# A two-layer diffusion step on one core: norms multiplied in by a diagonal matrix, one modulation unit moved between two layers, ring slots taken in the order in which they come free

## The chip, the cores and the metric

The kernel runs on one core of a Trainium2 chip. The metric is the device time of one execution in microseconds. Three executions of the kernel before took 1282.77, 1283.19 and 1284.61 us, median 1283.19 us. All data is fp32.

## The reference, cut to what matters

Two groups of 128 tokens (a prompt, t = 0, and a sample, t = 1) of width 1024 pass two layers. Each layer has an attention sub-layer and a mixture of 16 experts. Each sub-layer begins with an RMS norm whose result is shifted and scaled by values from a "modulation" product, and ends with a gated residual:

```
m   = silu(cond) @ w_mod[l] + b_mod[l]           # 6 x 1024: shift, scale, gate, twice
h   = x * rsqrt(mean(x*x) + eps) * g * (1 + scale) + shift
x   = x + gate * sublayer(h)                     # attention + projections, then top-2 of 16 experts
```

Weights are read once from HBM, 488 MB in all, most of it the experts' `w_gate`, `w_up` and `w_down`.

## The kernel before, in words

**Weights.** All weights go through a ring of six SBUF slots of 2 MB (`ring`, `SLOTS`). The dense units of a layer are listed by `dense_units(l)`: "mod" units (a quarter of the rows of `w_mod` for one group of 2048 columns), "in" units (512 columns of the input projection) and "out" units (512 columns of the output projection). SyncE issues their loads in that list's order (`load(g)`, L464 for a mod unit, L466 for the others). Unit g takes the slot of unit g - 6 and waits until TensorE has read that one (`read_at(g - SLOTS)`). The experts' units then take the same slots in turn: `load_first` (waits for the last six dense units), `load_early`, and the loops `load_in_turn`. Their DMAs are all issued at L475. The unit that TensorE has read is told by the semaphores `mod_used`, `filled` and `moe_used`.

**Order of the work.** TensorE works through one fixed order of jobs. In the dense part it is written out by hand in `FILL[l]`: at points called "head", "keys", "scores", and for each of the eight turns j of the attention before (`(j,)`) and after (`j`) its product with the values. Each turn is transposed probabilities (L699), scores of a later turn (L812), values (L849, L855 or L863). The items are ("in", u, t) = `project` (L752), ("wo", u, t) = `out_project` (L770), ("mod", l, group, k) = `mod` (L721, accumulated over k = 0..3 in one bank), ("hT", kind, t) = `norm`, ("rt", t) = `logits` (L875). Ahead of "head" the order is in the code: `project(l, 0, 1)`, `norm(l, 0, 0)`, then `project` of u = 1, 2, 3.

**A norm.** There are eight: (l, kind, t), kind 0 ahead of the attention and kind 1 ahead of the experts. ScalarE squares x and sums it (L1137 for 1024 columns at once; for (l, 1, 0) in two halves at L1133). VectorE asks for mean + eps (L1355, or L1386 and L1388 with halves). GpSimd raises it to the power -1/2 (L618). VectorE multiplies all of x by that number into scratch (`normed_rows`, L1395). TensorE transposes the scratch, eight 128x128 blocks into two PSUM banks (`norm`, which calls `transposes`, L699). ScalarE scales and shifts the first bank into `hT` (`modulate`, L1144) and VectorE the second (L1402). Only then can the product that reads `hT` start.

**Experts.** Eight pairs of experts per layer: `gather` (L932), `product` (L971), `scatter` (L941). The last pair is unrolled, with `last_product` and `last_scatter` (L1014). After it VectorE adds the four quarters (t, u) in `add_last`: a product with the gate (L1711, which counts `y_added`) and the sum into x (L1713, which counts `x_ready`).

**Between the layers.** VectorE runs `add_last` for (t = 1, u = 0), (1, 1), (0, 0), then asks for the norm of t = 1, then `add_last` of (0, 1), then `normed_rows(1, 0, 1)`, and the same for t = 0. ScalarE squares t = 1, then t = 0, and only then modulates t = 1. TensorE runs `mod(1, 1, 0)`, waits for `y_added` of all four quarters, and runs `norm(1, 0, 1)` and `project(1, 0, 1)`.

Of the kernel before, what the change touches and what calls it, by code (L numbers as in the profile page):

```python
# [12 lines left out]
D = 1024  # L13
# [89 lines left out]
def turn(l, j):  # L103
# [5 lines left out]
    0: {"head": [("in", 4, 1), ("in", 0, 0), ("in", 1, 0)],  # L109
# [13 lines left out]
    1: {"head": [("in", 4, 1), ("in", 5, 1)],  # L123
# [4 lines left out]
        2: [("mod", 1, 1, 1)],  # L128
        3: [("mod", 1, 1, 2), ("mod", 1, 1, 3)],
# [26 lines left out]
def dense_units(l):  # L156
# [4 lines left out]
    return shifts[0:1] + inputs + shifts[1:4] + scales[0:2] + out + scales[2:4]  # L161
# [14 lines left out]
def psum_jobs():  # L176

    names = [("vecT",), ("bT",)]
    for l in range(LAYERS):
# [7 lines left out]
        add( ("in", 0, 1), ("hT", 0, 0), ("in", 1, 1), ("in", 2, 1), ("in", 3, 1))  # L187
# [28 lines left out]
def build(nc, a):  # L216
    ctx = ExitStack()
    with ctx:
# [29 lines left out]
        ss = sb("ss", [P, 4])  # L248
# [111 lines left out]

        powers = {}
# [24 lines left out]
        N0 = len(dense_units(0))  # L386
        unit_no = {u: i for i, u in enumerate(units)}

        def dense_slot(g):

            return (g if g < N0 else g - OUTSIDE) % SLOTS

        MOE_AT = [N0 % SLOTS, dense_slot(len(units))]
# [23 lines left out]
        def read_at(g):  # L417

            if units[g][0] == "mod":
                l, group, k = units[g][1:]  # L420
                return mod_used, 12 * l + 4 * group + k + 1
            kind, l, u = units[g]
            return filled, fill({"in": ("qkv", l, u, 0), "out": ("wo", l, u, 0)}[kind])
# [34 lines left out]
        def _(sp):  # L458
# [9 lines left out]
            def experts(l):  # L468
# [8 lines left out]
                def load_in_turn(k, at, wait):  # L477
                    slot = (MOE_AT[l] - OUTSIDE + k) % SLOTS
# [4 lines left out]
                def load_early(n, k):  # L483
                    o = ring_turn(n, k)
                    slot = (MOE_AT[l] + o) % SLOTS
# [9 lines left out]
                def last_units(n):  # L495
# [4 lines left out]
                    for half in range(2):  # L500
                        for e in range(2):
                            k = MOE_UNITS - 2 + e
                            slot = (MOE_AT[l] - OUTSIDE + k) % SLOTS
# [88 lines left out]
            for g in range(N0, len(units)):  # L592
# [3 lines left out]
                else:  # L596
                    sp.wait_ge(*read_at(g - SLOTS))
# [80 lines left out]
        def _(pe):  # L678
# [241 lines left out]
            def experts(l):  # L920
# [23 lines left out]
                def product(n, k, banks, lhs, ready, half_done=None):  # L944
# [5 lines left out]
                    slots = [0, 0] if kept else [(MOE_AT[l] + turn_of + e) % SLOTS for e in range(2)]  # L950
# [883 lines left out]
```

## Time and profile before

| | |
|---|---|
| median of three executions | 1283.19 us |
| the profiled execution | 1283.81 us |
| its span | 1282.0 us |
| TensorE busy (PE) | 1183.7 us, 92% |
| VectorE, ScalarE, GpSimd busy | 279.4, 188.4, 49.4 us |
| bytes moved | 491.62 MB, mean 383 GB/s |
| matmuls of the experts' products (L971) | 638.6 us busy |

The span runs from the first to the last instruction; the execution's own time is 1.81 us longer. In 1 of the page (busy time by engine) PE is busy nearly all the time. In 2 of the page (40 slices) the DMA engines move about 427 GB/s in most slices, and far less in slices 2 and 3 and 21 to 24, the dense parts of the two layers.

### The profile page before, as it was taken

Reading aid. Unit: us, or ns where it says so; the run is one execution under the profiler, and the core shown is the slowest. Engines: PE = TensorE matmul, PEld = TensorE weight load, DVE = VectorE, ACT = ScalarE, POOL = GpSimd, SP = SyncE. Lnnn points to the kernel's source line nnn. Section 1 sums busy time; section 2 is a strip of 40 time slices with the busy share of each in tenths; the row PEclk is TensorE's granted clock in tenths of the full one; section 3 lists DMA queues with packets and bytes.
Section 4 is the critical chain, followed back from the end, with each engine's and each line's share of the span. In section 5 each row is a group of like instructions: output and inputs, shape, how many; then the busy total and the mean of one; then the engine's idle time right before and its main releaser. Section 6 shows DMA issues by size and latency. Waiting matters only on the chain.

```text
span 1282.0 us, 13868 instructions
## 1 busy us (share of the span) xinstructions
PE 1183.7 (92%) x5519; PEld 517.6 (40%) x5519; DVE 279.4 (22%) x672; ACT 188.4 (15%) x437; POOL 49.4 (4%) x57
## 2 busy tenths in 40 slices
PE   4999989999889898989899999999998899889898
PEld 2545454343333334333344554743433334343333
DVE  1156441201021010101413433412020110101013
ACT  1234221000000100000121342210000001000010
POOL 0502000000000000000011100000000000000000
PEclk9999999999999999999989999899999999999999
DMA  9959999999999999999991579889999999999995
GB/s 376 333 201 386 423 408 424 429 392 427 430 428 427 430 427 430 428 427 429 408 330 57 207 279 415 324 353 424 374 429 427 429 427 429 429 427 430 427 428 230
DMA packets 57647, 491.62 MB, mean 383 GB/s; under 512 B 5090, under 2 KB 6258, under 8 KB 26884
## 3 DMA queue, kind: packets, MB, share of 16 engines
q1 hardware_dynamic: 55408, 485.92, 91.4%
q0 software_dynamic: 2016, 4.94, 1.3%
q8 instruction: 29, 0.48, 0.1%
q10 hardware_dynamic: 180, 0.17, 0.0%
q14 instruction: 14, 0.11, 0.0%
HBM read 488.26 MB, written 2.75 MB: 383 GB/s over the span
## 4 chain that ended last, share of the span: by engine, by line
PE 72%; DMA 18%; issue 5%; DVE 2%; ACT 1%; SPq 1%; POOL 1%; DVEq 0%; ACTq 0%; POOLq 0%
PE bank L971 42%; DMA ring<-in_w_gate 11%; PE bank L752 11%; DMA ring<-in_w_up 5%; PE bank L770 3%; PE bank L941 3%; PE bank L932 3%; DMA ring<-in_w_in_ab 2%; PE bank L721 2%; PE bank L699 2%; PE bank L992 1%; PE bank L1021 1%; PE bank L812 1%; PE bank L1005 1%; PE bank L875 1%
## 5 line engine op out<-in xcount | busy, mean ns | idle before, releaser
L971 PE MATMUL bank<-ring,hT 128*64 128x512 f32 x2816 | 638.6, 608 | 63.7 <-issue 30.0
L971 PEld LDWEIGHTS bank<-ring,hT 128*64 128x64 f32 x2816 | 213.3, 140 | 464.5 <-issue 462.7
L752 PE MATMUL bank<-ring,hT 128*128 128x512 f32 (+1 forms) x352 | 149.5, 583 | 4.7 <-DMA ring<-in_w_in_ab 2.4
L752 PEld LDWEIGHTS bank<-ring,hT 128*128 128x128 f32 x352 | 67.1, 193 | 80.0 <-issue 76.6
L1694 DVE TENSOR_TENSOR work<-work,bank 128x512 f32<-128x512 f32 x56 | 38.5, 687 | 193.6 <-PE bank L941 193.4
L1687 DVE TENSOR_TENSOR work<-work,bank 128x512 f32<-128x512 f32 x32 | 22.0, 687 | 236.5 <-PE bank L971 236.5
L1728 DVE COPY work<-bank 128x512 f32<-128x512 f32 x16 | 11.1, 692 | 225.6 <-PE bank L971 209.3
L932 PE MATMUL bank<-work 128*128 128x128 f32 x512 | 59.8, 275 | 0.0
L932 PEld LDWEIGHTS bank<-work 128*128 128x128 f32 x512 | 58.6, 192 | 0.0
L770 PE MATMUL bank<-ring,work 128*128 128x512 f32 x128 | 56.3, 594 | 0.0
L1274 ACT ACTIVATE hT<-bank 128x512 f32<-128x512 f32 x32 | 19.0, 595 | 248.3 <-PE bank L1021 248.3
L941 PE MATMUL bank<-work 128*128 128x512 f32 x112 | 51.8, 605 | 0.0
L721 PE MATMUL bank<-ring,cond 128*32 128x512 f32 x384 | 47.0, 623 | 1.6 <-DMA ring<-in_w_mod 1.2
L1300 ACT ACTIVATE work<-bank 128x512 f32<-128x512 f32 x16 | 9.6, 597 | 220.3 <-PE bank L971 193.0
L1675 DVE TENSOR_TENSOR work<-work,bank 128x512 f32<-128x512 f32 x32 | 22.0, 688 | 83.4 <-ACT work L1283 83.4
L971 PE MATMUL bank<-work,hT 128*64 128x512 f32 x152 | 39.2, 593 | 0.0
L770 PEld LDWEIGHTS bank<-ring,work 128*128 128x128 f32 x128 | 23.8, 190 | 28.7 <-issue 28.6
L1287 ACT ACTIVATE work<-bank 128x256 f32<-128x256 f32 x16 | 6.2, 385 | 196.4 <-PE bank L1040 196.4
L1283 ACT ACTIVATE work<-bank 128x512 f32<-128x512 f32 x32 | 19.1, 597 | 94.5 <-PE bank L971 94.5
L941 PEld LDWEIGHTS bank<-work 128*128 128x128 f32 x112 | 20.1, 189 | 31.5 <-issue 31.5
L1211 ACT ACTIVATE work<-bank,nm 128x256 f32<-128x256 f32 (+1 forms) x64 | 26.1, 421 | 29.9 <-DVE nm L1486 29.9
L1420 DVE TENSOR_REDUCE hss<-bank 128x8 f32<-128x512 f32 (+1 forms) x16 | 10.5, 657 | 88.8 <-ACT bank L1170 88.8
(195 smaller groups left out, 688.5 us busy)
## 6 DMA issues: line engine op xcount, KB each, us to landing
ring<-in_w_gate SPq DMA_DIRECT2D x64, 2048.0 KB, 17.0
ring<-in_w_up SPq DMA_DIRECT2D x56, 2048.0 KB, 17.2
ring<-in_w_down SPq DMA_DIRECT2D x56, 2048.0 KB, 16.9
ring<-in_w_mod SPq DMA_DIRECT2D x23, 2048.0 KB, 11.9
work<-in_w_up SPq DMA_DIRECT2D x8, 2048.0 KB, 17.8
ring<-in_w_in_c SPq DMA_DIRECT2D x6, 2048.0 KB, 20.2
ring<-in_w_in_ab SPq DMA_DIRECT2D x4, 2048.0 KB, 21.5
ring<-in_w_down SPq DMA_DIRECT2D x8, 1024.0 KB, 16.3
```

What stands on the lines that cost most here:

```text
L699: ins = pe.transpose(b[:, i * P:(i + 1) * P], src, K("ident"))
L721: ins = pe.matmul(out, cond[:, 2 * k + r, :], cols, start=(k, r) == (0, 0), stop=(k, r) == (3, 1), tile_position=(0, 32 * j))
L752: ins = pe.matmul(b[:, 0:n], hT[:, c, t * P:(t + 1) * P], w[:, c, 0:n], start=c == 0, stop=c == DC - 1)
L770: ins = pe.matmul(b[:, :], oT(l, t, c), w[:, c, :], start=c == 0, stop=c == DC - 1)
L932: ins = pe.matmul(bank[h][:, c * P:(c + 1) * P], htok(t)[:, at:at + P], pick[:, t, :], start=t == 0, stop=t == 1)
L941: pe.matmul(bank[4 + 2 * t + h][:, :], GT[:, t, :], yd[:, h * UC:(h + 1) * UC], start=True, stop=True).then_inc(m["scattered"], 1)
L971: ins = pe.matmul(bank[banks[j]][64 * e:64 * e + 64, :], lhs[:, 4 * h + c, 64 * e:64 * e + 64], weights(e, c, j), start=(h, c) == (0, 0), ...
L1211: ins = act.activation(PR[:, j % 2, h, 0:nk], bank_of(("S", l, t, b, e))[:, i * nk:(i + 1) * nk], ACT.Exp, bias=nm[:, j % 2, h:h + 1], sca ...
L1283: act.activation(sg[:, h * UC:(h + 1) * UC], bank[h][:, :], ACT.Sigmoid).then_inc(m["sig_done"], 1)
L1675: dve.tensor_tensor(hid[:, half], sg[:, half], bank[h][:, :], ALU.mult).then_inc(m["gate_taken"], 1)
L1687: dve.tensor_tensor(hid[:, half], hid[:, half], bank[2 + h][:, :], ALU.mult).then_inc(m["hid_done"], 1)
L1694: dve.tensor_tensor(y[:, t, cols], y[:, t, cols], bank[4 + 2 * t + h][:, :], ALU.add).then_inc(m["y_added"], 1)
```

## The change: what it does

1. `norm` on TensorE no longer transposes scratch. It multiplies: the block of x is the stationary operand, and a 128x128 diagonal matrix with the tokens' factors is the moving one. `normed_rows` on VectorE makes only that matrix, from the identity.
2. `mod(1, 1, 1)` moves from turn 2 of layer 1 to the point between `norm(1, 0, 1)` and `project(1, 0, 1)`, and its load from eighth to third place in the list of layer 1. The jobs ahead of "head" become a point "front" of `FILL`.
3. The squares of (1, 0, 1) are made in halves too. VectorE makes that norm's factors and diagonal ahead of the quarters of t = 0.
4. A slot is taken in the order in which TensorE gives slots back (`released`), not in the order in which they were loaded; the same for the experts' first six units.

```diff
@@ FILL
-    0: {"head": [("in", 4, 1), ("in", 0, 0), ("in", 1, 0)],
+    0: {"front": [("in", 0, 1), ("hT", 0, 0), ("in", 1, 1), ("in", 2, 1), ("in", 3, 1)],
+        "head": [("in", 4, 1), ("in", 0, 0), ("in", 1, 0)],
...
-    1: {"head": [("in", 4, 1), ("in", 5, 1)],
+    1: {"front": [("mod", 1, 1, 1), ("in", 0, 1), ("hT", 0, 0), ("in", 1, 1), ("in", 2, 1), ("in", 3, 1)],
+        "head": [("in", 4, 1), ("in", 5, 1)],
...
-        2: [("mod", 1, 1, 1)],
-        3: [("mod", 1, 1, 2), ("mod", 1, 1, 3)],
+        2: [("mod", 1, 1, 2)],
+        3: [("mod", 1, 1, 3)],
@@ dense_units
-    return shifts[0:1] + inputs + shifts[1:4] + scales[0:2] + out + scales[2:4]
+    return shifts[0:1] + inputs[0:1] + shifts[1:2] + inputs[1:] + shifts[2:4] + scales[0:2] + out + scales[2:4]
+def released(l):
+    order = [("mod", 0, 0, k) for k in range(4)] if l == 0 else [("mod", 1, 1, 0)]
+    for point in points(l):
+        for item in FILL[l].get(point, []):
+            if item[0] == "mod":
+                order.append(item)
+            elif item[0] in ("in", "wo") and item[2] == 0:
+                order.append(("in" if item[0] == "in" else "out", l, item[1]))
+    return order
@@ slots
+        HALVED = [(0, 1, 0), (1, 0, 1), (1, 1, 0)]
+            for i, u in enumerate(mine):
+                place[u] = first[i] if i < SLOTS else place[free_order[l][i - SLOTS]]
+            MOE_RING.append([place[u] for u in free_order[l][-SLOTS:]])
+        def room_for(g):
+            return read_at(free_order[0][g - SLOTS] if g < N0 else free_order[1][g - N0 - SLOTS])
@@ SyncE, load_first
-                    slot = (MOE_AT[l] + k) % SLOTS
-                    sp.wait_ge(*read_at((N0 if l == 0 else len(units)) - SLOTS + k))
+                    slot = moe_slot(l, k)
+                    sp.wait_ge(*read_at(free_order[l][k - SLOTS]))
@@ SyncE, dense loads
-                    sp.wait_ge(*read_at(g - SLOTS))
+                    sp.wait_ge(*room_for(g))
@@ TensorE
             def norm(l, kind, t):
                 pe.wait_ge(xn_ready, 4 * l + 2 * kind + 2 - t)
                 for h in range(2):
-                    transposes(("hT", l, kind, t, h), [channels(xn(kind, t), 4 * h + i) for i in range(4)])
+                    name = ("hT", l, kind, t, h)
+                    b = bank_free(name)
+                    for i in range(4):
+                        ins = pe.matmul(b[:, i * P:(i + 1) * P], channels(x[:, t, :], 4 * h + i), xn(kind, t)[:, 0:P], start=True, stop=True)
+                    ins.then_inc(filled, 1)
...
                 if l == 1:
                     norm(1, 0, 1)
-                project(l, 0, 1)
-                norm(l, 0, 0)
-                for u in range(1, 4):
-                    project(l, u, 1)
+                meanwhile(l, "front")
@@ ScalarE, norm
-                if (kind, t) == (1, 0):
+                if halved(l, kind, t):
                     for u in range(2):
-                        act.wait_ge(x_ready, done - 1 + u)
-                        act.activation(xn(1, 0)[:, u * UC:(u + 1) * UC], x[:, 0, u * UC:(u + 1) * UC], ACT.Square,
-                                       accum_out=ss[:, 3 * u:3 * u + 1]).then_inc(half_squares if u == 0 else ssq_ready, 1)
+                        act.wait_ge(x_ready, done - 1 - 2 * t + u)
+                        at = t + 4 * u
+                        act.activation(xn(kind, t)[:, u * UC:(u + 1) * UC], x[:, t, u * UC:(u + 1) * UC], ACT.Square,
+                                       accum_out=ss[:, at:at + 1]).then_inc(half_squares if u == 0 else ssq_ready, 1)
@@ VectorE
             def normed_rows(l, kind, t):
                 taken(("norm", l, kind, t))
-                dve.tensor_scalar(xn(kind, t), x[:, t, :], ss[:, t:t + 1], None, ALU.mult).then_inc(xn_ready, 1)
+                dve.tensor_scalar(xn(kind, t)[:, 0:P], K("ident"), ss[:, t:t + 1], None, ALU.mult).then_inc(xn_ready, 1)
...
                 add_last(end, 0, 1)
                 add_last(end, 1, 1)
-                add_last(end, 0, 0)
                 if l == 0:
                     norm_asked(1, 0, 1)
+                    normed_rows(1, 0, 1)
+                add_last(end, 0, 0)
                 add_last(end, 1, 0)
                 if l == 0:
-                    normed_rows(1, 0, 1)
                     norm_asked(1, 0, 0)
                     normed_rows(1, 0, 0)
```

`norm_asked` on VectorE takes the halves for every norm in `HALVED`. ScalarE's and VectorE's own calls ahead of the attention become `meanwhile(l, "front")` in the same order as before. The order of TensorE's other jobs is unchanged.

## Rows read from the trace of the kernel before

**Rows 1.** The page: its first line, and GB/s in 40 slices of 32 us.

```profile
span 1282.0 us, 13868 instructions
...
GB/s 376 333 201 386 423 408 424 429 392 427 430 428 427 430 427 430 428 427 429 408 330 57 207 279 415 324 353 424 374 429 427 429 427 429 429 427 430 427 428 230
```

**Rows 2.** Stretches: each engine's busy time, PEclk, DMA share, GB/s; experts of both layers.

```profile
280.00:288.00 8.00, 8.00 (x40) 2.73 (x38) 0.69 (x1) 0.60 (x1) 0.00 (x0) 1.00 0.90 344
...
920.00:928.00 8.00, 8.00 (x40) 2.67 (x38) 0.69 (x1) 0.60 (x1) 0.00 (x0) 1.00 0.86 334
```

**Rows 3.** Timeline of SyncE's DMA issues: start us, us, what.

```profile
268.81 13.05 SPq L475 DMA_DIRECT2D ring<-in_w_gate  x4
```

**Rows 4.** Chain that ended last: start us, us, what.

```profile
38.25 0.89 PE bank L699 x8
...
186.73 3.57 PE bank L932 x32
```

**Rows 5.** Timeline: start us, us, what, idle before it; start of the kernel.

```profile
29.25 1.50 ACT L1144 ACTIVATE hT<-bank,modc 128x128 f32<-128x128 f32 x4 [1.56 <-DVE modc L1380]
...
31.11 7.13 PE L752 MATMUL bank<-ring,hT 128*128 128x512 f32 x16 [2.40 <-DMA ring<-in_w_in_ab]
...
63.35 0.22 DVE L1782 TENSOR_SCALAR early<-early 128x128 f32<-128x128 f32 x1
```

**Rows 6.** Timeline: norm (0, 1, 0) and the logits behind it.

```profile
171.42 0.63 ACT L1133 ACTIVATE tmp<-x 128x512 f32<-128x512 f32 x1 [6.96 <-DVE x L1538]
...
173.08 0.75 DVE L1395 TENSOR_SCALAR tmp<-x,ss 128x1024 f32<-128x1024 f32 x1 [0.67 <-POOL ss L618]
173.89 1.15 PE L699 MATMUL bank<-const,tmp 128*128 128x128 f32 x8 [2.17 <-DVE tmp L1395]
...
176.82 1.96 PE L875 MATMUL bank<-wr,hT 128*128 128x16 f32 x16
```

**Rows 7.** Timeline: between the layers.

```profile
637.13 1.92 PE L721 MATMUL bank<-ring,cond 128*32 128x512 f32 x16
...
637.44 1.06 ACT L1137 ACTIVATE work<-x 128x1024 f32<-128x1024 f32 x1 [3.23 <-DVE x L1713]
...
638.72 0.69 DVE L1711 TENSOR_TENSOR tmp<-bank,gbuf 128x512 f32<-128x512 f32 x1
638.88 0.55 POOL L618 TENSOR_TENSOR ss<-ss,const 128x1 f32<-128x1 f32 x1 [465.83 <-DVE ss L1355]
...
640.95 1.14 PE L699 MATMUL bank<-const,work 128*128 128x128 f32 x8 [1.89 <-DVE work L1395]
...
642.84 1.36 DVE L1402 TENSOR_SCALAR hT<-bank,modc 128x128 f32<-128x128 f32 x4
...
644.35 10.16 PE L752 MATMUL bank<-ring,hT 128*128 128x512 f32 x16 [2.26 <-DVE hT L1402]
```

**Rows 8.** DMA issue and landing: size, us from issue to landing (issues of 617.39, 617.88).

```profile
617.88 0.61 SPq L466 DMA_DIRECT2D ring<-in_w_in_c  x1
...
ring<-in_w_in_c SPq DMA_DIRECT2D x1, 2048.0 KB, 22.0
```

**Rows 9.** Stretches with the granted clock: behind norm (1, 0, 1) and norm (1, 1, 0).

```profile
644.00:648.00 4.00, 3.65 (x5) 1.62 (x6) 0.20 (x1) 0.00 (x0) 0.00 (x0) 0.50 1.05 386
...
816.00:820.00 4.00, 4.00 (x20) 4.00 (x20) 0.78 (x5) 0.69 (x3) 0.00 (x0) 0.50 1.08 441
```

**Rows 10.** Timeline: turns 2 and 3 of layer 1.

```profile
753.53 0.21 ACT L1211 ACTIVATION_READ_ACCUMULATOR work<-bank,nm 128x1 f32 x1
...
754.96 1.08 ACT L1222 ACTIVATE work<-bank 128x512 f32<-128x512 f32 x2 [1.21 <-PE bank L699]
...
756.18 1.09 PE L863 MATMUL bank<-work 128*64 128x128 f32 x16 [0.18 <-ACT work L1222]
```

**Rows 11.** Timeline: norm (1, 1, 0) and the logits behind it.

```profile
812.35 1.15 PE L699 MATMUL bank<-const,tmp 128*128 128x128 f32 x8 [1.42 <-DVE tmp L1395]
...
815.08 3.57 PE L875 MATMUL bank<-wr,hT 128*128 128x16 f32 x16 [1.58 <-ACT hT L1144]
```

More of the change, by code:

```diff
@@ L186, in psum_jobs @@
             add(("modT", 0))
-        add( ("in", 0, 1), ("hT", 0, 0), ("in", 1, 1), ("in", 2, 1), ("in", 3, 1))
+        add(*FILL[l]["front"])
         add(*FILL[l]["head"])
@@ L386, in build, with moe_slot @@
         N0 = len(dense_units(0))
+        mods_used = {u: i + 1 for i, u in enumerate(u for l in range(LAYERS) for u in released(l) if u[0] == "mod")}
         unit_no = {u: i for i, u in enumerate(units)}
+        free_order = [released(l) for l in range(LAYERS)]
+        place, MOE_RING = {}, []
+        for l in range(LAYERS):
+            first = list(range(SLOTS)) if l == 0 else [MOE_RING[0][(i - OUTSIDE) % SLOTS] for i in range(SLOTS)]
+            mine = dense_units(l)
+            assert sorted(mine) == sorted(free_order[l])
+            for i, u in enumerate(mine):
+                place[u] = first[i] if i < SLOTS else place[free_order[l][i - SLOTS]]
+            MOE_RING.append([place[u] for u in free_order[l][-SLOTS:]])
         def dense_slot(g):
-            return (g if g < N0 else g - OUTSIDE) % SLOTS
-        MOE_AT = [N0 % SLOTS, dense_slot(len(units))]
+            return place[units[g]]
+        def moe_slot(l, k):
+            return MOE_RING[l][k % SLOTS]
         projected = [("qkv", l, u, t) for l in range(LAYERS)
@@ L415, in squares_of, with read_at @@
             return projected.index(name) + 1
[L417 to L422, printed above, removed]
+        def room_for(g):
+            return read_at(free_order[0][g - SLOTS] if g < N0 else free_order[1][g - N0 - SLOTS])
+        def read_at(unit):
+            if unit[0] == "mod":
+                l, group, k = unit[1:]
+                return mod_used, mods_used[unit]
+            kind, l, u = unit
             return filled, fill({"in": ("qkv", l, u, 0), "out": ("wo", l, u, 0)}[kind])
@@ L477, in load_in_turn @@
                 def load_in_turn(k, at, wait):
-                    slot = (MOE_AT[l] - OUTSIDE + k) % SLOTS
+                    slot = moe_slot(l, k - OUTSIDE)
                     sp.wait_ge(moe_used[l], wait)
@@ L484, in load_early @@
                     o = ring_turn(n, k)
-                    slot = (MOE_AT[l] + o) % SLOTS
+                    slot = moe_slot(l, o)
                     sp.wait_ge(moe_used[l], OUTSIDE + o + 1)
@@ L502, in last_units @@
                             k = MOE_UNITS - 2 + e
-                            slot = (MOE_AT[l] - OUTSIDE + k) % SLOTS
+                            slot = moe_slot(l, k - OUTSIDE)
                             src = a["w_down"][l].rearrange("e k n -> (e k n)")[at[e]:at[e] + D * D].rearrange("(h p r) -> h p r", h=2, p=P)[1]
@@ L949, in product @@
                     apart = kept and (n, k) == (0, SLOTS + 2)
-                    slots = [0, 0] if kept else [(MOE_AT[l] + turn_of + e) % SLOTS for e in range(2)]
+                    slots = [0, 0] if kept else [moe_slot(l, turn_of + e) for e in range(2)]
                     h = k // 2 % 2
@@ L984, in last_product @@
                     k = MOE_UNITS - 2
-                    slots = [(MOE_AT[l] - OUTSIDE + k + e) % SLOTS for e in range(2)]
+                    slots = [moe_slot(l, k + e - OUTSIDE) for e in range(2)]
                     pe.wait_ge(m["ht_ready"], 2 * n + 2)
@@ L1321, in _ @@
                     norm(0, 0, 0)
-                project(l, 0, 1)
-                modulate(l, 0, 0)
-                for u in range(1, 4):
-                    project(l, u, 1)
+                meanwhile(l, "front")
                 if l == 0:
@@ L1771, in _ @@
                     normed_rows(0, 0, 0)
-                project(l, 0, 1)
-                modulate(l, 0, 0)
-                for u in range(1, 4):
-                    project(l, u, 1)
+                meanwhile(l, "front")
                 qk_asked(l, 1)
```

19 lines of the change are left out of this document (12 added, 7 removed).

## The prediction

> **What bounds the kernel now.** I read the stretches first, then SyncE's issues, then the timelines around the eight norms and between the layers. Deep in the experts the DMA moves about 427 GB/s [rows 1] and nothing else matters: the weights still to come set the time. Before that there is in each layer a last moment at which the DMA engines run dry because all slots are full: 344 and 334 GB/s in the stretches that begin at 280 and 920 [rows 2]. In layer 0 SyncE issues again at 268.81, when TensorE has given a slot back [rows 3], and TensorE is busy 8.00 of 8.00 us there. So each layer's end moves with TensorE's progress up to its second pair of experts (to about 285 and 922). After that only bytes count, and the change moves no bytes. A microsecond added to or taken from TensorE's path in the dense parts goes to the end; a load that comes earlier is worth nothing unless TensorE waited for it. The profiled execution took 1283.81 us (span 1282.0 [rows 1] and 1.81 around it), 0.62 above the median of 1283.19. The sum is made against 1283.81.
>
> **A norm on TensorE.** Eight transposes are eight records and take 0.89 us; the gather's 16 plain 128x128 products are 32 records and take 3.57 us [rows 4], 0.223 each. A plain fp32 product thus costs two passes where a transpose costs one. Eight products with the diagonal: 8 x 0.223 = 1.79, +0.90 us per norm. The scratch that was transposed had the same stride between columns as x has, so I add nothing for that. Bounds: 0 (as fast as a transpose) and +0.90; I take +0.90, since the gather's row has the same shape and type.
>
> The Trainium skill, "TensorE: Matmul & The Clock Gate", section "Terms", speaks against the change more strongly: it calls the transpose mode four times faster for fp32. By that a product would take 0.44 us and a norm 2.7 us more. Rows 4 show a factor of two, and the measurement decides.
>
> **A norm on VectorE.** The factors are now multiplied into 128 columns (0.22 us for that size [rows 5]) and not 1024 (0.75 [rows 6]): -0.53, which counts only where TensorE waits for it.
>
> **Layer 0.**
> - (0, 0, 1): TensorE's +0.90 comes ahead of the modulation's last product, so the scale and shift (29.25 to 30.75) ends at 31.65. The first projection started at 31.11, released by its load [rows 5]: that covers 0.36. I take +0.6. If the load were late anyway, 0; if the cover fails, +0.90.
> - (0, 0, 0), at 38.25 between two projections: TensorE has no gap, +0.90 [rows 4].
> - (0, 1, 1), at 152: again no gap, +0.90. (This is the pattern of four norms: at 38, 152, 654 and 793.)
> - (0, 1, 0): TensorE waited 2.17 us for VectorE [rows 6]. -0.53 and +0.90 = +0.36. The unit mod(1, 0, 2) behind it hides the scale and shift as before.
> Sum +2.76. The experts' first unit takes its slot one unit earlier, but TensorE waits for no load there, and DMA is saturated (423, 408, 424 and 429 GB/s from 128 to 256 [rows 1]): nothing.
>
> **Between the layers** [rows 7]. Before: ScalarE squares x of t = 1 from 637.44, 1.06 and 0.19 for the sum; request; power 0.55 from 638.88; VectorE first finishes a quarter, then makes the rows; TensorE starts at 640.95. After: the second half square takes 0.63 [rows 6] + 0.19, to 638.25; request and power to 639.0; diagonal ready 639.25, some 1.6 earlier than the rows were. But TensorE also waits for `y_added` of all four quarters, and VectorE now makes the quarters of t = 0 behind the diagonal. The last of the gate products (L1711) moves from 638.72 to 639.27 + 2 x 0.70 = 640.67 and ends 641.36. So TensorE starts the norm at 641.4, 0.45 later than before, and is through at 643.2. x of t = 0 is complete at 642.08; ScalarE squares it in one piece (to 643.35) ahead of its own modulation, VectorE makes the second diagonal (to 644.3) and then its modulation, 1.36 long: hT ready at 645.7, against 644.2 before. By itself the reordering costs 1.5 us.
> Into that gap goes mod(1, 1, 1), 1.85 us to the next job's start. Its load stands behind in_w_in_c's first unit, issued 617.88, landed 22.0 later at 639.9 [rows 8]. 2.1 MB at 427 GB/s are 4.9 us: landed 644.8. So mod 644.8 to 646.65, and the projection starts there, 2.3 later than 644.35. Behind the waiting mod on TensorE stands everything.
> The clock: behind the old gaps (1.89 and 2.26 us, with nothing but eight transposes between them) the granted clock was 0.50 in 644 to 648, the lower of the two levels (1.2 GHz), and the projection took 10.16 us [rows 7, 9], against 7.13 [rows 5]: 3.0 lost. The new gaps are 2.35 (639.05 to 641.4) and 1.6, with 1.8 us of real products between. Ahead of norm (0, 1, 0) one gap of 2.17 us did not bring the clock down [rows 6]. So I take it that it holds: the projection ends 646.65 + 7.0 = 653.65 against 654.5, -0.85. If it falls, +2.0.
>
> **Rest of layer 1.**
> - (1, 0, 0): no gap, +0.90.
> - mod(1, 1, 1) gone from turn 2: 1.85 less on TensorE. Then values of turn 3 wait for ScalarE: its exponentials end at 753.74, two copies of 1.08 in all end at 754.85, values start at 755.0 where they started at 756.18 [rows 10]: -1.18. The rest becomes a wait.
> - (1, 1, 1): TensorE runs on without a gap into the output projections, +0.90.
> - (1, 1, 0): +0.36 as in layer 0. But here the clock was down as well (0.50 in 816 to 820 [rows 9]) after gaps of 1.42 and 1.58 us round the transposes, and the logits took 3.57 us [rows 11] against 1.96 [rows 6], on the path to the router. Now the gaps are 0.87 and 1.6 round 1.8 us of products: I take it that the clock holds, -1.7. Bounds -1.7 and 0.
> - Loads earlier by one unit: TensorE waits for no load in the dense part of layer 1, and the slots are full again before the experts' first product is done: nothing.
> Sum -0.85 + 0.90 - 1.18 + 0.90 + 0.36 - 1.7 = -1.57.
>
> **Total** +2.76 - 1.57 = +1.2: 1285.0 us, 1.8 over the median.
>
> **Rivals.**
> 1. *The clock falls between the layers all the same* (slower, 22%). For: the first gap is now longer (2.35). Against: real products fill the middle. The mod takes up to 3.7 us at half clock and the projection is slow to about 650.5: 2.0 to 3.0 more, 1287.0 to 1288.0. It decides if the longer gap alone is enough, whatever follows it.
> 2. *The added load is late* (slower, 6%): TensorE stands at mod(1, 1, 1) until the whole queue has passed in_c's second unit, 5 us later. With no clock lost +2, with it +5: about 1288.
> 3. *Layer 0's additions do not reach the end* (no change, 15%): the dry stretch at 280 comes from something other than slots. Against: rows 3. Then -1.57 alone, 1282.2.
> 4. *A product with a diagonal is as cheap as a transpose* (faster, 14%). The +0.90s go: layer 0 -0.53, between the layers -0.85, -1.18, -0.53, -1.7 = -4.8, 1279.0. Against: rows 4, squarely.
> 5. *The reordering does not do what it says*: it is in the forecast, since the first norm starts later and not earlier.
>
> **How the numbers follow.** Forecast 43%, own range 1283.8 to 1286.4. What measurements of this kernel tell from no change is about 0.2%, 2.6 us: below 1280.6 is faster, above 1285.8 slower. Slower: a quarter of the forecast (0.11), nearly all of rivals 1 and 2 (0.28): 0.39. Faster: rival 4, 0.14. Within: the remaining 0.47. The range for 8 in 10 leaves out rival 4 and the far end of rivals 1 and 2: 1281.0 to 1288.0.
>
> **What would show it.** L699 gone from the eight norms, and in its place 16 records of 128x128 in 1.8 us each time. TensorE's norm between the layers 0.45 us later against the end of `last_scatter`, released by L1711 and not by the diagonal. mod(1, 1, 1) released by its load. PEclk 1.00 from the end of the experts to the first projection, and 1.00 around the last logits. Values of turn 3 waiting about 1 us for ScalarE. First pair of layer 0 2.8 us later, and the dry stretch at 280 later by as much. The prediction is wrong if a norm takes 0.9 us, if hT is ready before the mod's weights by more than a microsecond, or if the clock reads 0.50 in both places.

## The result, and the profile after

The changed kernel takes 1301.47 us (median of 4 runs, 1301.20 to 1302.11); the kernel before took 1282.98 us beside it (4 runs, 1280.53 to 1284.61). The ratio is 1.0151, 95% interval 1.0136 to 1.0165: slower by 18.5 us. Forecast were 1285.0 us and a range of 1281 to 1288. The profiled execution of the changed kernel took 1301.5 us.

The first line of its page, and its GB/s in 40 slices (32.5 us each), against [rows 1]:

```profile
span 1299.7 us, 14000 instructions
...
GB/s 375 322 167 346 415 422 358 424 398 405 429 431 428 428 428 428 428 427 428 417 392 51 259 226 392 321 258 424 373 431 427 428 429 429 429 428 428 429 429 247
```

The same plateau at 428, the same hollows in the dense parts, one more dip (358, slice 6 counted from 0). The experts' sections take no longer than before (table below); the time is lost ahead of them. There the eight norms stand out. The new products stand in L781 (L738 are now the transposes): count, least/median/greatest duration in ns, first and last start.

```profile
L781 PEld LDWEIGHTS bank<-work,x x64: 312/336/343, 24.3 to 669.6; 128*128 128x128 f32 x64
L781 PE MATMUL bank<-work,x x64: 272/402/605, 24.3 to 669.7; 128*128 128x128 f32 x64
L781 PEld LDWEIGHTS bank<-tmp,x x64: 312/336/340, 159.8 to 831.2; 128*128 128x128 f32 x64
```

128 records for 64 products are two passes each, as forecast. But a weight load (LDWEIGHTS, of the stationary operand) takes 336 ns and a pass 402 (medians), where the transposes of the attention (L738 on `work`) show 140 and 273. In the chain that ended last (start us, us, what) the norms and their neighbours are:

```profile
24.40 4.12 PE bank L781 x16
...
34.08 8.80 PE bank L796 x16
42.89 3.68 PE bank L781 x16
46.57 37.79 PE bank L796 x96
...
159.88 4.02 PE bank L781 x16
163.90 6.87 PE bank L814 x16
...
183.81 4.19 PE bank L781 x16
188.00 2.35 PE bank L760 x16
```

Compare 42.89 with the first row of [rows 4]: the same place, between two projections without a gap, 3.68 us where it was 0.89.

Between the layers, timeline of TensorE, against [rows 7]:

```profile
645.56 3.70 PE L1058 MATMUL bank<-work 128*128 128x512 f32 x8
649.19 1.92 PE L760 MATMUL bank<-ring,cond 128*32 128x512 f32 x16
653.42 4.11 PE L781 MATMUL bank<-work,x 128*128 128x128 f32 x16 [2.30 <-DVE tmp L1752]
657.46 1.92 PE L760 MATMUL bank<-ring,cond 128*32 128x512 f32 x16
659.31 7.13 PE L796 MATMUL bank<-ring,hT 128*128 128x512 f32 x16
```

The norm waits 2.30 us for the gate product on VectorE and not for the diagonal, the moved modulation unit needs no wait, and the projection runs at full clock: 7.13 us and not 10.16. And the last norm with its logits, against [rows 9, 11], first the timeline, then the stretches (the number ahead of the DMA share is the granted clock):

```profile
827.68 4.19 PE L781 MATMUL bank<-tmp,x 128*128 128x128 f32 x16 [0.95 <-DVE tmp L1436]
833.45 3.57 PE L919 MATMUL bank<-wr,hT 128*128 128x16 f32 x16 [1.58 <-issue]
```

```profile
828.00:832.00 4.00, 3.87 (x16) 3.58 (x15) 0.02 (x1) 1.50 (x4) 0.00 (x0) 0.50 1.01 354
832.00:836.00 4.00, 2.55 (x12) 2.58 (x13) 1.35 (x4) 0.00 (x0) 0.00 (x0) 0.50 0.98 414
836.00:840.00 4.00, 4.00 (x20) 4.00 (x21) 2.24 (x11) 1.56 (x4) 0.00 (x0) 0.50 0.98 409
```

Here the clock stood at 0.50 as before, and the logits took the same 3.57 us.

A ledger of the delay against the kernel before, from the starts of the same jobs in the two timelines: first projection +2.97 (34.08 against 31.11 [rows 5]); second projection +7.43; layer 0's last output projection +10.38; behind norm (0, 1, 0) +12.96; last scatter of layer 0 +12.06; end of layer 1's first projection +11.94; logits of t = 0 in layer 1 +18.37; end of the span +17.7.

### The profile page after: what moved, and what is told of

Read it like the earlier page. It is cut to its first block, busy times and chain, and to the rows that moved or that the text cites. A ratio compares the mean times of both kernels' runs of the same rounds, so it can differ in the third digit from the quotient of the medians.

```text
span 1299.7 us, 14000 instructions
## 1 busy us (share of the span) xinstructions
PE 1205.6 (93%) x5583; PEld 539.3 (41%) x5583; DVE 276.2 (21%) x673; ACT 188.7 (15%) x439; POOL 49.4 (4%) x57
## 4 chain that ended last, share of the span: by engine, by line
PE 73%; DMA 18%; issue 5%; DVE 2%; ACT 1%; POOL 1%; SPq 0%; DVEq 0%; POOLq 0%; ACTq 0%
PE bank L1015 41%; PE bank L796 11%; DMA ring<-in_w_up 10%; DMA ring<-in_w_gate 6%; PE bank L976 3%; PE bank L814 3%; PE bank L985 2%; PE bank L760 2%; PE bank L781 2%; DMA ring<-in_w_mod 2%; PE bank L738 1%; PE bank L1036 1%; PE bank L1065 1%; PE bank L856 1%; PE bank L787 1%
```

## The experiments

Each was run 4 to 12 times beside the kernel before (median there 1281.74, 1281.61 and 1281.87 us in the three sets), except e0, e10 and e11, which are one execution each. "A", "B - A", "C - B" and "D" are sections of the profiled span: to the start of layer 0's first gather, on to layer 0's last scatter, on to layer 1's first gather, on to the end. They are read from the starts of three groups in TensorE's timeline. The kernel of e0 is the kernel before up to layer 1's last scatter, so its first three sections are a third profile of that kernel:

```
kernel, profiled execution     span     A      B - A    C - B    D
before                        1282.0  186.57  446.93   192.91  455.59
before again (e10)            1282.4  192.40  445.49   190.44  454.07
before, with e0's products         -  188.26  444.67   194.23       -
after                         1299.7  200.01  445.55   199.73  454.41
diagonal only (e3)            1302.2  200.51  445.46   201.54  454.69
after, transposes (e1)        1276.5  186.44  445.42   190.57  454.07
after, no factor (e6)         1279.2  187.91  445.86   191.55  453.88
slots only (e4)               1279.4  188.38  444.50   192.33  454.19
slots, moved unit (e2)        1278.2  188.10  445.32   190.52  454.26
unit further ahead (e7)       1283.1  191.19  445.48   190.67  455.76
fillers (e8)                  1279.6  192.44  445.44   188.25  453.47
fillers again (e11)           1274.1  186.62  445.61   188.25  453.62
fillers, moved unit (e9)      1281.2  190.66  445.51   190.95  454.08
```

**e3: the diagonal alone.** To the kernel before:

```diff
-                    transposes(("hT", l, kind, t, h), [channels(xn(kind, t), 4 * h + i) for i in range(4)])
+                    name = ("hT", l, kind, t, h)
+                    b = bank_free(name)
+                    for i in range(4):
+                        ins = pe.matmul(b[:, i * P:(i + 1) * P], channels(x[:, t, :], 4 * h + i), xn(kind, t)[:, 0:P], start=True, stop=True)
+                    ins.then_inc(filled, 1)
...
-                dve.tensor_scalar(xn(kind, t), x[:, t, :], ss[:, t:t + 1], None, ALU.mult).then_inc(xn_ready, 1)
+                dve.tensor_scalar(xn(kind, t)[:, 0:P], K("ident"), ss[:, t:t + 1], None, ALU.mult).then_inc(xn_ready, 1)
```

> The kernel before with the norms multiplied in by the diagonal and nothing else. Theory: each norm 2.8 to 3.2 us more on TensorE, 0.5 saved on VectorE where it is waited for: 1303 to 1306 us, more than the changed kernel, since the moved unit is not there to fill the gap. Rival (the moved unit's wait or the slot order carries a part of the loss): below 1297.

1303.62 us (4 runs, 1302.25 to 1303.99), ratio 1.0169 [1.0151, 1.0188]. The diagonal alone costs at least about as much as the whole change (1.0151 [1.0136, 1.0165]; the intervals overlap).

**e1: everything but the diagonal.** The two edits of e3 undone in the changed kernel:

```diff
-                        ins = pe.matmul(b[:, i * P:(i + 1) * P], channels(x[:, t, :], 4 * h + i), xn(kind, t)[:, 0:P], start=True, stop=True)
+                    transposes(("hT", l, kind, t, h), [channels(xn(kind, t), 4 * h + i) for i in range(4)])
...
-                dve.tensor_scalar(xn(kind, t)[:, 0:P], K("ident"), ss[:, t:t + 1], None, ALU.mult).then_inc(xn_ready, 1)
+                dve.tensor_scalar(xn(kind, t), x[:, t, :], ss[:, t:t + 1], None, ALU.mult).then_inc(xn_ready, 1)
```

> The changed kernel with one part undone: VectorE multiplies whole rows again and TensorE transposes them. Theory (the eight norms' products are the loss, directly and by the clock): back to 1281 to 1285 us; between the layers the norm starts 0.9 us later than in the kernel before and the projection 2.5 us later, the unit of modulation no longer in turn 2 gives back 1.7. Rival (slot order, moved unit or VectorE's order hold a share of the loss): above 1290.

1281.29 us (12 runs), ratio 0.9998 [0.9987, 1.0009]. So the loss is the diagonal's, and the rest of the change is worth nothing that these runs can tell. Against the changed kernel's profile it is 13.57 us shorter in A and 9.16 in C - B, and within 0.4 in the two sections without a norm. 1.67 of A is the first projection's clock (7.13 us here, 8.80 there), and 0.5 that of the modulation unit behind norm (0, 1, 0) (1.92 and 2.42).

**e0: the price of the product by itself.** Nine groups of products and transposes on data at hand, behind layer 1's last scatter of the kernel before; one execution, 1325.62 us. The stationary operand is the one that LDWEIGHTS loads, the moving one is the MATMUL's other input; a column stride of s means that neighbouring columns lie s elements apart. In order: 16 products with a contiguous stationary operand (L1084), 16 each with a column stride of 2, 4 and 8 elements (L1086, L1088, L1090), 16 transposes at stride 8 and contiguous (L1092, L1094), 16 products with the moving operand at stride 8 (L1096), 8 products of 512 columns with the stationary one at stride 8 and contiguous (L1098, L1100):

```diff
+                    part = lambda c, s: flat_h.rearrange("r (p c) -> r c p", c=s)[:, c % s, 0:P]
+                    for c in range(16):
+                        pe.matmul(bank[0][:, 0:P], flat_h[:, (c % 8) * P:(c % 8 + 1) * P], K("ident"), start=True, stop=True)
...
+                    for c in range(16):
+                        pe.matmul(bank[0][:, 0:P], part(c, 8), K("ident"), start=True, stop=True)
+                    for c in range(16):
+                        pe.transpose(bank[0][:, 0:P], part(c, 8), K("ident"))
...
+                    for c in range(16):
+                        pe.matmul(bank[0][:, 0:P], K("ident"), part(c, 8), start=True, stop=True)
+                    for c in range(8):
+                        pe.matmul(bank[0][:, :], part(c, 8), flat_h[:, 0:512], start=True, stop=True)
```

> The kernel before with nine groups of unneeded work on TensorE behind the last scatter of layer 1, each group alone: 16 plain 128x128 products with the stationary operand's columns contiguous, then 16 with columns 2, 4 and 8 elements apart, 16 transposes with columns 8 apart, 16 transposes contiguous, 16 products with a contiguous stationary and a moving operand 8 apart, 8 products of 512 columns with stationary 8 apart and 8 contiguous. Theory (the stride of the stationary operand is what made the norms' products slow): contiguous 3.6 us (0.11 per record), 8 apart 7.4 us (0.23 per record, as in the changed kernel), transposes 1.8 us with either stride, moving operand 8 apart 3.6 us, 512 columns 7.0 us with either, since the load hides behind the longer product. Rival (a plain fp32 product always costs four transposes, so the gather's row was the exception): all four plain groups 7.4 us. Second rival (operands freshly written by other engines made it slow): 3.6 us for all four plain groups here.

The lines; least/median/greatest ns, first and last start:

```profile
L1084 PEld LDWEIGHTS bank<-const,hT x32: 190/192/192, 1275.8 to 1279.6; 128*128 128x128 f32 x32
L1084 PE MATMUL bank<-const,hT x32: 272/275/275, 1276.2 to 1279.7; 128*128 128x128 f32 x32
...
L1086 PE MATMUL bank<-const,hT x32: 281/281/282, 1279.8 to 1283.5; 128*128 128x128 f32 x32
...
L1088 PE MATMUL bank<-const,hT x32: 396/397/397, 1283.6 to 1290.8; 128*128 128x128 f32 x32
L1090 PEld LDWEIGHTS bank<-const,hT x32: 334/335/336, 1290.9 to 1298.3; 128*128 128x128 f32 x32
L1090 PE MATMUL bank<-const,hT x32: 401/402/403, 1291.1 to 1298.4; 128*128 128x128 f32 x32
...
L1092 PE MATMUL bank<-const,hT x16: 272/273/277, 1298.7 to 1300.3; 128*128 128x128 f32 x16
...
L1094 PE MATMUL bank<-const,hT x16: 272/272/273, 1300.4 to 1302.1; 128*128 128x128 f32 x16
...
L1096 PE MATMUL bank<-hT,const x32: 393/412/413, 1302.2 to 1309.4; 128*128 128x128 f32 x32
...
L1098 PE MATMUL bank<-hT x16: 591/592/612, 1309.6 to 1316.1; 128*128 128x512 f32 x16
...
L1100 PE MATMUL bank<-hT x16: 592/593/593, 1316.5 to 1322.9; 128*128 128x512 f32 x16
```

First to last start, divided by the intervals between records, times the records of one product: 0.226 us for a contiguous stationary operand (31 intervals, two records), 0.24 at a column stride of 2 elements, 0.46 at 4, 0.47 at 8. A transpose takes 0.11 in either layout. With 512 moving columns the stride costs nothing (0.87 against 0.85). The expectation that a moving operand with stride 8 would cost no more than a contiguous one was wrong: 0.46. The medians of the L1090 rows are those of the L781 rows of the changed kernel to within 1 ns. 8 x 0.47 = 3.76, and the chain has 3.68 to 4.19 for a norm.

**e5: the same products with contiguous columns in the changed kernel.**

```diff
-channels(x[:, t, :], 4 * h + i), xn(kind, t)[:, 0:P], start=True, stop=True)
+x[:, t, (4 * h + i) * P:(4 * h + i + 1) * P], xn(kind, t)[:, 0:P], start=True, stop=True)
```

> The changed kernel with one size changed: the norms' products read 128 neighbouring columns of x as stationary operand where they read every eighth (so the channels stand in another order in hT than the weights expect; the work is the same as long as the router still fits its experts into one round). Theory (the stride is the whole of the miss, and the rest of the forecast's sum holds): each norm 1.8 us on TensorE, and the time is the forecast's own, 1.2 over the profiled execution of before or 1 to 4 us over the median of the kernel before beside it: 1282.5 to 1286. Rival (products also bring the clock down where transposes did not, or the moved unit's order costs by itself): 1288 or more.

The channels come in another order, so other numbers reach the router, and one more round over the experts was run: 1756.84 us, which compares with nothing. Up to layer 0's first gather the work is the same. Its line, and two places of its chain:

```profile
L781 PEld LDWEIGHTS bank<-work,x x64: 186/192/337, 24.3 to 1127.3; 128*128 128x128 f32 x64
L781 PE MATMUL bank<-work,x x64: 272/275/422, 24.3 to 1127.4; 128*128 128x128 f32 x64
```

```profile
40.58 1.78 PE bank L781 x16
...
155.66 1.98 PE bank L781 x16
...
177.55 2.05 PE bank L781 x16
```

1.78 us is the 8 x 0.223 of the forecast. The first gather starts at 191.12, 4.55 us behind the kernel before, where the forecast's layer 0 said 2.76. The difference lies ahead of the first projection, which starts 2.37 us later where 0.6 was forecast: the first norm took 3.35 us in a stretch with 0.59 granted (24 to 28). Behind it the three norms add 0.85, 0.91 and 0.43 us to TensorE's starts, against 0.90, 0.90 and 0.36 forecast. So in layer 0 the forecast's other terms hold once the columns are contiguous; the rest of it this run can't test.

**e6: a transpose by the identity, the factor left out.** The form that rival 4 priced:

```diff
-ins = pe.matmul(b[:, i * P:(i + 1) * P], channels(x[:, t, :], 4 * h + i), xn(kind, t)[:, 0:P], start=True, stop=True)
+ins = pe.transpose(b[:, i * P:(i + 1) * P], channels(x[:, t, :], 4 * h + i), K('ident'))
```

> The changed kernel with the identity in place of the diagonal and transposes in place of products: the factors of the norms are left out of hT, all waits and the short work on VectorE stay. It gives what the change would be worth if a diagonal cost TensorE no more than a transpose. Theory (the prediction's rival 4): 3 to 5 us faster than the kernel before. Rival (the short work on VectorE buys nothing, since other waits end last): as e1_transposed, within 1 us of before.

1281.6 us (10 runs), ratio 1.0011 [0.9984, 1.0037]. The waits are those of the change. Even with the products at a transpose's price, the 128 columns on VectorE instead of 1024 give no gain that shows. Rival 4's 1279.0 is not reached.

**e4, e2, e7: the slots, the moved unit, and the unit further ahead.** e4 is the kernel before with the slots taken in the order of release. e2 adds mod(1, 1, 1) ahead of the projection, and its load in third place. e7 puts it behind mod(1, 1, 0) instead, and its load in second place:

```diff
@@ e4 to e2
+    1: {"front": [("mod", 1, 1, 1), ("in", 0, 1), ...
-        2: [("mod", 1, 1, 1)],
@@ e2 to e7
-    1: {"front": [("mod", 1, 1, 1), ("in", 0, 1), ...
-    return shifts[0:1] + inputs[0:1] + shifts[1:2] + inputs[1:] + shifts[2:4] + ...
+    return shifts[0:2] + inputs + shifts[2:4] + ...
                     mod(1, 1, 0)
+                    mod(1, 1, 1)
```

> The kernel before with the slot order of the change and nothing else. Theory: TensorE waits for no load in the dense parts, so earlier loads are worth nothing: within 0.5 us of before, and SyncE issues the experts' first units earlier in the trace. Rival (an earlier start of the experts' loads fills the dry stretch and shortens the run): 1 us or more under before.

1281.49 us (10 runs), ratio 0.9997 [0.9983, 1.0012]. SyncE issued the first load of the experts' `w_gate` into the ring at 156.87 instead of 160.42, and that bought nothing.

> The same, and VectorE's order between the layers and the whole square of (1, 0, 1) are those of before: left are the slot order and the moved modulation unit. Theory: TensorE starts the norm as in the kernel before (7.4 us after the start of the last scatter), then waits for the moved unit's load and runs it, projection 2.3 us later than before; if the granted clock then reads 1.00 through the projection 1280 to 1281 us, if it reads 0.50 there 1283 to 1284. Rival (VectorE's new order is worth something): slower than e1_transposed.

1280.56 us (12 runs), ratio 0.9994 [0.9982, 1.0006].

> e2_mod_only with the moved unit one place further ahead, in TensorE's order (right behind mod(1, 1, 0), ahead of the norm) and in the load order (second, ahead of the first input unit). Theory: the unit fills the wait for the quarters and the norm, which has 1.9 us in it and takes 1.85, its load is there 5 us earlier (it lands before the scatter's end plus 3), the first input unit lands just when hT is ready; the projection starts as in the kernel before or up to 0.5 us later, and 1.85 are saved later: layer 1 from last scatter to its second product 2 us shorter than before, median 2 to 4 us under before. Rival (the input unit, now third, lands later than hT): projection 2 us later, no gain over e2_mod_only.

1282.81 us (12 runs), ratio 1.0004 [0.9991, 1.0017]. Three times nothing measurable; none of the gains expected for e7 shows. The timeline of e2 shows what the moved unit meets once the norm is short again:

```profile
640.88 1.25 PE L738 MATMUL bank<-const,work 128*128 128x128 f32 x8 [1.90 <-DVE work L1432]
643.91 3.64 PE L760 MATMUL bank<-ring,cond 128*32 128x512 f32 x16 [1.79 <-DMA ring<-in_w_mod]
647.48 7.66 PE L792 MATMUL bank<-ring,hT 128*128 128x512 f32 x16
```

It waits 1.79 us for its load, which landed at 643.87 (forecast: 644.8), and then runs at half clock, 3.64 us: rival 1's picture. In the changed kernel neither is to be seen: the unit starts at 657.46, right behind the slow norm and without a wait. In e7 the unit waits for nothing, and the projection behind it waits 2.27 us for VectorE and starts at 647.52, at a clock of 0.57.

**e8, e9: fillers where TensorE stands idle.** The kernel has a filler already (`keep_busy`, a product of the identity with itself). e8 is the kernel before with more of them; e9 is e1 with the same but the eight ahead of the projection:

```diff
+        BUSY_NORM = {(1, 0, 1): 7, (1, 1, 0): 5}    # into the norm's bank, ahead of its wait
+        BUSY_PROJECT = {(1, 0, 1): 8}               # into the projection's bank
...
             def logits(l, t):
+                if (l, t) == (1, 0):
+                    pe.wait_ge(mod_emptied, 6)
+                    keep_busy(6)
```

> The kernel before, to which short products of the constant identity (128x128, the kernel's own filler, 0.22 us at full clock) are added where TensorE stands idle around the last norms: 7 ahead of norm (1,0,1) and 8 ahead of layer 1's first projection (idle 1.89 and 2.26 us there), 5 ahead of norm (1,1,0) and 6 ahead of its logits (idle 1.42 and 1.58 us). Nothing of the change is in it. Theory (the clock of the stretches behind these gaps is set by TensorE's idling, and it is this, not the order of the modulation units, that could bring time there): layer 1's first projection takes 7.1 us and not 10.16, the last logits 1.85 and not 3.57, their transposes 1.07 and not 1.95, the fillers behind them 2.6 to 3.0 and not 3.29 to 3.49; of these about 3 us between the layers and 2.5 to 4 us at the logits reach the end, and the median falls by 3 to 6 us to 1276 to 1279, ratio 0.995 to 0.998. Rival (the clock returns a fixed while after a gap whatever stands in it, or short products do not hold it): the granted clock stays 0.50 in 644:648 and 812:820, and the median stays within 0.1% of before. Second rival (the fillers end after the work they wait for and delay it): the norm's transposes start later than 2.0 us behind the last filler's start and the median rises by 0.5 to 1 us.

1281.15 us (12 runs, 1276.01 to 1286.11), ratio 0.9994 [0.9978, 1.0011]. Locally it is as the theory says; timeline, then stretches:

```profile
648.73 7.10 PE L761 MATMUL bank<-ring,hT 128*128 128x512 f32 x16 [0.39 <-DVE hT L1414]
...
816.44 1.93 PE L887 MATMUL bank<-wr,hT 128*128 128x16 f32 x16 [0.24 <-issue]
...
823.12 0.40 PE L900 MATMUL bank<-chosen,const 128*128 128x16 f32 x2 [1.16 <-DVE chosen L1617]
```

```profile
644.00:648.00 4.00, 4.00 (x37) 4.00 (x38) 2.78 (x7) 2.66 (x6) 0.55 (x1) 1.00 1.05 386
...
816.00:820.00 4.00, 3.76 (x34) 3.60 (x34) 1.36 (x8) 1.21 (x5) 0.00 (x0) 1.00 1.02 399
```

The clock is 1.00 in both places, the projection takes 7.10 us, the logits 1.93. The section C - B is 188.25; only its own repetition is as short. The median does not show the 3 to 6 us expected.

> The changed kernel with whole rows and transposes in place of the diagonal (so slots, moved modulation unit and the halves stay), with the same fillers but without those ahead of the projection, where the moved unit stands: 7 ahead of norm (1,0,1), 5 ahead of norm (1,1,0), 6 ahead of its logits. Theory: between the layers there is little left to hold (the projection took 7.1 us already where the unit had landed), so it stands within 0.1% of the kernel before with fillers; against the kernel before 3 to 5 us are gained at the last logits and in the steadier clock between the layers, 1276 to 1279. Rival (fillers do not change the clock): 1281.3, as without them. Rival (moved unit and fillers add up): 1 us below the kernel before with fillers.

1282.52 us (12 runs), ratio 0.9999 [0.9985, 1.0014]. The fillers ahead of norm (1, 0, 1) stand behind the wait of 2.76 us here, and so could not fill it; in the stretch from 644 the clock was 0.57. The logits took 1.93 us at 1.00, but behind them, where no filler was added, the last eight of the kernel's own fillers took 3.08 us and the gather 4.36 (2.03 and 3.74 in e8).

**e10, e11: second profiles**, one execution each, of the kernel before and of e8 unchanged.

> The kernel before once more, for a second profile of it: how much of a difference between two single profiles is the granted clock of that execution. By the profiles so far the section from the last scatter of layer 0 to the first gather of layer 1 (192.91 us in the kernel before, 190.5 with the modulation unit moved, 188.25 with fillers) is the same in every execution if only the code sets it: 192.9, within 0.3. If its clock differs by execution, it can come out as low as 190.5, and then the 2.4 us of the moved unit are not shown. The start up to layer 0's first gather (186.57) goes up to 188.3 where the first projection runs at half clock (8.8 and not 7.13 us).

1284.2 us. C - B is 190.44 and not 192.91, and in e0's profile, with the same code up to there, it was 194.23. So the 2.4 us that the moved unit seems to bring in this section are within what executions of one kernel differ. This profile's logits took 2.17 us and not 3.57:

```profile
818.39 2.17 PE L875 MATMUL bank<-wr,hT 128*128 128x16 f32 x16 [1.58 <-ACT hT L1144]
```

And its start took 192.40 instead of 186.57, with the first projection at 9.96 us.

> The kernel with fillers once more, for a second profile: the section from the last scatter to the first gather of layer 1 again 188.2 to 188.6 with a granted clock of 1.00 at the last logits (the fillers set it), the start up to the first gather somewhere from 187 to 192.5 by its clock. If instead the section comes out at 190 or more, the fillers do not hold the clock and the first profile was luck.

1275.92 us, C - B again 188.25 to the hundredth. So with fillers this section was the same both times, 2.2 to 6.0 us shorter than in the kernel before's three profiles. That A is 186.62 here and 192.44 in e8 is the execution's, not the code's. Why twelve runs have a median only 0.7 us lower stays open; the interval reaches down to 2.8 us less, so a gain of 2 us would not contradict it. As measured, no version here is faster than the kernel before.

## Why the prediction was wrong

**The step that failed** is "The scratch that was transposed had the same stride between columns as x has, so I add nothing for that." The term for the stride, put at nothing, is 1.9 us a norm: eight products took 3.68 us where 1.79 was forecast. The conclusion was drawn from an operation that does not show the cost. e0 has the four cases side by side: transposes do not mind the stride (0.11 and 0.11 us), products do (0.226 and 0.47). e5 has the same products in the changed kernel with contiguous columns, at 1.78 us a norm. The gather's row [rows 4] had the same shape and type but contiguous columns. The bounds, "0 (as fast as a transpose) and +0.90", thus left out a doubling; the rows of before had no strided 128-column product at all, and the upper bound should have said so.

**The factor of four that was set aside.** The Trainium skill ("TensorE: Matmul & The Clock Gate", section "Terms") calls the transpose mode four times faster for fp32. The estimate of +2.7 us a norm that the prediction worked out from it came out, +2.8 between the projections. As a statement on all operands the factor does not hold: with contiguous ones e0 has a factor of two (0.226 against 0.11 us), and four only with the strided ones (0.47 against 0.11). The measurement decides, but the row must have the operands' layout too.

**The sum with the right term.** Eight norms at 3.7 us, not 1.79, are 8 x 1.9 = 15.2 more. The clock that did not return at the last logits is 1.7. 1285.0 + 15.2 + 1.7 = 1301.9; the profiled execution took 1301.5. That it fits to 0.4 is in part luck. Layer 0 took 3.1 more than its terms give (13.44 against 2.76 + 4 x 1.9), 2.2 of it in the clock of the first projection and of the unit behind the last norm. Against that, 1.2 less was lost between the layers, 0.5 more gained in turn 3, and the experts gave back 1.4 in layer 0 and 0.7 behind the last logits. Norm by norm, what each put on the path:

```
                                 forecast   measured (change of the delay of TensorE's starts, after less before)
(0,0,1)                            +0.6      +2.97  first projection starts
(0,0,0)                            +0.90     +4.46  of it +2.79 the norm, +1.67 the first projection's clock
(0,1,1)                            +0.90     +2.95
(0,1,0)                            +0.36     +2.58
layer 0, to its first pair         +2.76    +13.44  0.48 of it mod(1,0,2) at a lower clock
between the layers, projection's end -0.85   -0.12
(1,0,0)                            +0.90     +2.80
mod(1,1,1) gone from turn 2        -1.18     -1.71
(1,1,1)                            +0.90     +2.83
(1,1,0), and the clock             -1.34     +2.51  start of the logits; they take 3.57 as before
```

**That layer 0's additions reach the end** (against rival 3) was right: of the 13.44, 12.06 are still there at the last scatter, and D differs by 1.2 between the two profiles. The dry stretch came where it was looked for, later and with a lower rate: 306 GB/s in the eight us from 280, and still 334 from 288, where the kernel before had 426 again. SyncE's issue of [rows 3] moved from 268.81 to 282.25, by the same 13.44. The issue, and the stretch at 280 against [rows 2]:

```profile
282.25 12.69 SPq L514 DMA_DIRECT2D ring<-in_w_gate  x4
...
280.00:288.00 8.00, 8.00 (x58) 5.56 (x56) 0.69 (x1) 2.28 (x4) 0.00 (x0) 1.00 0.80 306
```

**Between the layers** the order of events was right: the norm starts 0.41 later against the last scatter (forecast 0.45), released by the gate product, and the clock of the projection held. What holds it is in part open, but other runs show what was there when it held. First e3, with the same slow products and no unit, then e1, with the unit and transposes:

```profile
652.96 4.14 PE L741 MATMUL bank<-work,x 128*128 128x128 f32 x16 [1.43 <-DVE work L1399]
658.73 10.17 PE L756 MATMUL bank<-ring,hT 128*128 128x512 f32 x16 [1.63 <-DVE hT L1406]
```

```profile
642.37 2.44 PE L760 MATMUL bank<-ring,cond 128*32 128x512 f32 x16 [0.22 <-DMA ring<-in_w_mod]
645.07 7.10 PE L792 MATMUL bank<-ring,hT 128*128 128x512 f32 x16 [0.26 <-DVE hT L1439]
```

The slow products alone did not hold the clock: in e3 it was 0.50 in 656 to 660. With the unit the projection took 7.10 us (e1), 7.66 (e2) and 8.01 (e6), with the unit ahead of the norm 8.80 (e7), without it there 10.16, 10.04 (e0), 9.06 (e10) and 8.51 (e4). So the unit in the gap, which I credited, goes with a shorter projection in these single profiles, though inside the gap the clock fell all the same (0.57 in 640 to 644 in e1, 0.50 in 644 to 648 in e2). The gain at the end of the projection is small, because the projection starts later: from the start of the last scatter to the job behind the projection it is 20.15 us in e1, and 20.84, 20.73 and 19.75 in the kernel before's three profiles. A gain of 0.85 can't be told from that. The unit's wait for its load, also forecast, was covered by the slow norm.

**Turn 3** gave 1.71 where 1.18 was forecast. I had looked for a new wait for ScalarE of about 1 us. There was none: the values of turn 3 waited 0.18 us, as before. The diff moved mod(1, 1, 2) into turn 2, ahead of that wait, and what turn 3 lost was a unit behind it: a line of the diff not followed. On VectorE the diagonal took 0.29 us where 0.22 was read from [rows 5], so that TensorE's wait at (0, 1, 0) fell by 0.46 and not 0.53.

**The clock at the last logits** was forecast to return, and did not. Its reason was the same as between the layers, and e0 and e10 show that a single profile is no basis for it: one code, 3.57, 3.56 and 2.17 us. Of the ten profiles here without fillers (e5 left out) one has the logits at full clock (e2, 1.93 us); the three with fillers (e8, e9, e11) all have 1.93. So fillers go with the full clock in three of three, and without them it differs from execution to execution.

## What to carry to other kernels

Before a transpose is turned into a product, look at the column stride of what becomes the operand: with 128 moving columns, a stride of 4 elements or more doubled the product here, on top of the doubling against the transpose. A row is a price only for its shape, type and layout; if the layout is not in the trace, the upper bound must be open. And of a gain of 2 us in 1280, a section of one profile says nothing before a second profile of the same kernel has been laid beside it: one section of the kernel before took 190.4, 192.9 and 194.2 us.

## What the hardware showed that I had not expected

- The cost of the stride appears between 2 elements (0.24 us) and 4 (0.46) and hardly grows to 8 (0.47). It is the same for the moving operand (0.46), and gone behind 512 columns. What lies between 2 and 4, and other element sizes, were not tried.
- Strided products hardly feel the clock. Of two norms ahead of the experts, the one from 159.88 takes 4.02 us with 1.00 granted and the one from 827.68 4.19 with 0.50. Of two norms ahead of the attention, the one from 42.89 takes 3.68 with 1.00 and the first 4.12 with 0.59, where with the contiguous columns of e5 the same two take 1.78 with 1.00 and 3.35 with 0.58.
- The start (A) of one kernel takes 186.6, 188.3 or 192.4 us in the three profiles of the kernel before, and 186.6 or 192.4 with fillers. The granted clock differs with it: where A is 186.6 in the kernel before, it is 1.00 from 24 to 40 and from 176 to 184; where A is 192.4, it is 0.58 in 24 to 28, 0.50 in 32 to 36, 0.71 in 36 to 40 and 0.78 to 0.79 in 176 to 184.
